# Attention output projection: operands split into a rounded part and a remainder, in two passes over the token tiles, with half sums kept in memory between the passes

## The reference

```python
def attention_mixer(hn, w_in, sink, w_out):
    proj = hn @ w_in                       # q, k, v, gate
    ...
    o = windowed_gqa_sink(q, k, v, sink)   # 16 heads in 4 groups, |t-s| <= 128
    o = (o * jax.nn.silu(gate.astype(jnp.float32))).astype(hn.dtype)
    return o @ w_out                       # 1024 x 1024 times 1024 x 1024
...
for i in range(DEPTH):
    p = layer_params[i]
    hn = rms_norm(x, p[0])
    if i % N_MIXERS == 0:
        x = x + attention_mixer(hn, *p[1:])
    else:
        x = x + deltanet_mixer(hn, *p[1:])
return rms_norm(x, final_norm)
```

## Time and profile before

| | |
|---|---|
| median of 3 runs | 1385.36 us (1385.02 to 1390.39) |
| span of the profiled execution | 1388.3 us |
| PE busy | 1324.7 us, 95% |
| DVE, ACT, POOL busy | 815.0, 684.5, 237.5 us |
| output projection on PE (L1722) | from 372.2 to 517 us of the span |

### The profile page before, as it was taken

How to read it: one execution, slowest core, us unless ns; L and a number is a source line. 1 busy time by engine, 2 the same in 40 slices (tenths; PEclk the granted TensorE clock), 3 DMA queues, 4 the chain that set the end, 5 groups by cost and what they waited for, 6 DMA issues and landing times.

```text
span 1388.3 us, 25735 instructions
## 1 busy us (share of the span) xinstructions
PE 1324.7 (95%) x9981; PEld 982.5 (71%) x9981; DVE 815.0 (59%) x2284; ACT 684.5 (49%) x1757; POOL 237.5 (17%) x164
## 2 busy tenths in 40 slices
PE   5999999999999997889999999999999999998998
PEld 4866766667644445678888888888888888865543
DVE  6335444445345426785768777787777777743243
ACT  6155464564444433437376473664746646443121
POOL 7211010111001122204032030220311303100000
PEclk9999999999999999889999999999999999999999
DMA  5110011120211122001111021110201101053121
GB/s 189 31 46 25 22 31 31 32 76 31 92 58 50 46 78 77 31 17 47 32 47 47 22 72 32 47 47 17 77 32 47 47 17 62 1 212 107 31 76 76
DMA packets 19416, 74.81 MB, mean 54 GB/s; under 512 B 3040, under 2 KB 3296, under 8 KB 17760
## 3 DMA queue, kind: packets, MB, share of 16 engines
q1 hardware_dynamic: 19296, 73.18, 15.5%
HBM read 61.04 MB, written 12.12 MB: 53 GB/s over the span
## 4 chain that ended last, share of the span: by engine, by line
PE 86%; DVE 6%; ACT 4%; issue 2%; DMA 2%; POOL 0%; SPq 0%; DVEq 0%; POOLq 0%
PE bank L1747 21%; PE bank L1650 17%; PE bank L1722 8%; PE bank L1787 4%; PE bank L1677 4%; PE bank L1762 3%; PE bank L1703 3%; PE bank L1688 3%; PE bank L1921 2%; PE bank L1839 2%; PE bank L1846 2%; PE bank L1935 2%; PE bank L1872 2%; PE bank L1938 2%; PE bank L1821 2%; PE bank L1820 2%
## 5 line engine op out<-in xcount | busy, mean ns | idle before, releaser
L1747 PE MATMUL bank<-hn_hi,w_hi 128*128 128x512 f32 x512 | 223.4, 436 | 0.5 <-ACT arena L1044 0.5
L1747 PE MATMUL bank<-hn_hi,w_lo 128*128 128x512 f32 x512 | 202.5, 396 | 0.0
L1747 PE MATMUL bank<-hn_lo,w_hi 128*128 128x512 f32 x512 | 201.3, 393 | 0.0
L1650 PE MATMUL bank<-hn_hi,w_hi 128*128 128x512 f32 x320 | 136.6, 427 | 0.5 <-ACT arena L979 0.2
L1650 PE MATMUL bank<-hn_hi,w_lo 128*128 128x512 f32 x320 | 125.8, 393 | 0.0
L1650 PE MATMUL bank<-hn_lo,w_hi 128*128 128x512 f32 x320 | 125.6, 392 | 0.0
L1722 PE MATMUL bank<-arena 128*128 128x512 f32 x256 | 119.0, 598 | 0.0
L919 POOL TENSOR_TENSOR w_lo<-arena,w_hi 128x1024 fp32r<-128x1024 f32 x24 | 61.4, 2559 | 321.8 <-ACT w_hi L1075 321.8
L1747 PEld LDWEIGHTS bank<-hn_hi,w_lo 128*128 128x128 f32 x512 | 96.8, 189 | 22.3
L1258 DVE CUSTOM_DVE_ANT_0 arena<-bank,arena 128x384 f32<-128x384 f32 (+1 forms) x128 | 70.1, 581 | 67.1 <-issue 66.8
L1747 PEld LDWEIGHTS bank<-hn_hi,w_hi 128*128 128x128 f32 x512 | 97.6, 191 | 16.4 <-ACT arena L1044 0.7
(11 more groups left out here) (234 smaller groups left out, 2653.9 us busy)
## 6 DMA issues: line engine op xcount, KB each, us to landing
arena<-in_w SPq DMA_DIRECT2D x52, 512.0 KB, 3.6
arena<-in_x SPq DMA_DIRECT2D x16, 512.0 KB, 4.7
arena<-gc_scratch SPq DMA_DIRECT2D x8, 1024.0 KB, 5.1
x_scratch<-arena SPq DMA_DIRECT2D x8, 512.0 KB, 2.6
arena<-x_scratch SPq DMA_DIRECT2D x8, 512.0 KB, 3.7
out<-arena SPq DMA_DIRECT2D x8, 512.0 KB, 2.6
oT_scratch<-arena SPq DMA_DIRECT2D x7, 512.0 KB, 5.2
arena<-oT_scratch SPq DMA_DIRECT2D x7, 512.0 KB, 8.2
```

The costliest lines, as they stand in the source:

```text
L1650: ins = te.matmul(bank[r % 2][:], wp[:, tile % 2, k], hp[:, k, hf * HALF:(hf + 1) * HALF], start=(k == 0 and m == 0), stop=(k == KT - 1 an ...
L1747: ins = te.matmul(b[:], wp[:, t % 2, k], hp[:, k, hf * HALF:(hf + 1) * HALF], start=(k == 0 and m == 0), stop=(k == KT - 1 and m == 2))
```

## The change

The output projection is made with split operands: `ornd` (ACT) copies a tile of four rows of `oT` to `oT_hi`, a ring of three; `osplit` (POOL) writes the remainder over the plain values; `wornd` and `wosplit` do the same for the eight rows of the output weights; and an item is now three fp32r matmuls. The split weights take up memory that was free before only in part: rows 0 to 3 lie in the columns of `hn_hi` and `hn_lo` of tokens 0 to 511, from the end of group 2's share of the projections on, and rows 4 to 7 in the split buffers of the input weights and in the ring of their loads.

The tiles are gone over twice (`OP_SEQ`): part 0 takes rows 0 to 3 of tiles 3, 4, 5, 6, 7, 0, 1, 2, part 1 takes rows 4 to 7 of tiles 0 to 7. So each tile has four `add`s in place of two (32 in place of 16). The half sums of tiles 3 to 7 are stored to `x1_scratch` and loaded again. `sq`, `nrm`, `ntr` and what follows now hang on part 1, with 8 items per tile: `nrm` of the tile before stands behind item 4, `ntr` behind items 6 and 8. The `Sqrt` moves from the event `sq` to the event `nrm`. `nout` writes straight into the place of `hn_lo`, `nlo` works in place, and the wait of `nout` for `nlo` is gone.

```diff
@@ -395,23 +399,31 @@
...
-            def op_items(t):
-                orders = [(hf, j) for hf in range(2) for j in (4, 5, 6, 7, 0, 1, 2, 3)]
-                if t == 0:
-                    orders = [(hf, j) for j0 in (4, 0) for hf in range(2) for j in range(j0, j0 + 4)]
-                items = [[("op", t, hf, j)] for hf, j in orders]
-                seen = [0, 0]
-                for it, (hf, j) in zip(items, orders):
-                    seen[hf] += 1
-                    if seen[hf] == KT:
-                        it.append(("add", t, hf))
-                items[-1].append(("sq", 1, t))
-                if t >= 1:
-                    items[4].append(("nrm", 1, t - 1))
-                    items[8] += [("ntr", 1, t - 1, 0), ("nout", 1, t - 1, 0), ("nhi", 1, t - 1, 0), ("nlo", 1, t - 1, 0)]
-                    items[11] += [("ntr", 1, t - 1, 1), ("nout", 1, t - 1, 1), ("nhi", 1, t - 1, 1), ("nlo", 1, t - 1, 1)]
+            def op_items(part, t):
+                items = [[("op", part, t, hf, j)] for hf in range(2) for j in range(4 * part, 4 * part + 4)]
+                for hf in range(2):
+                    items[4 * hf + 3].append(("add", part, t, hf))
+                if part == 0:
+                    after = OP_SEQ.index((0, t)) + 2
+                    if after < NT:
+                        items[-1] += [("ornd", after), ("osplit", after)]
+                else:
+                    items[-1].append(("sq", 1, t))
+                    if t >= 1:
+                        items[3].append(("nrm", 1, t - 1))
+                        items[5] += [("ntr", 1, t - 1, 0), ("nout", 1, t - 1, 0), ("nhi", 1, t - 1, 0), ("nlo", 1, t - 1, 0)]
+                        items[7] += [("ntr", 1, t - 1, 1), ("nout", 1, t - 1, 1), ("nhi", 1, t - 1, 1), ("nlo", 1, t - 1, 1)]
                 return items
+            def late_op(t):
+                split = [("ornd", NT + t), ("osplit", NT + t)]
+                if stream:
+                    stream[max(0, len(stream) - 8)] += split
+                else:
+                    put(*split)
+                stream.extend(op_items(1, t))
...
@@ -425,8 +437,14 @@
...
                     quota, share = 16, (2, 2, 2, 2, 3)
-                if 2 <= B - (A_GROUPS - 1) * NT < NT + 1:
-                    stream += op_items(B - (A_GROUPS - 1) * NT - 2)
+                late = B - (A_GROUPS - 1) * NT
+                if late == 1:
+                    put(*[(what, i) for i in range(2) for what in ("ornd", "osplit")])
+                if late == 2:
+                    for part, t in OP_SEQ[:NT]:
+                        stream.extend(op_items(part, t))
+                if 2 <= late < NT + 1:
+                    late_op(late - 2)
...
@@ -438,6 +456,9 @@
...
                     put(("exp", B))
+                    if late in (0, 1, 3, 4):
+                        for j in {0: (0, 1), 1: (2, 3), 3: (4, 5), 4: (6, 7)}[late]:
+                            put(("wornd", j), ("wosplit", j))
...
@@ -768,15 +825,25 @@
...
             sp.wait_ge(xn_done, NT)
-            for t in range(XR):
-                sp.dma_start(xr[:, t, :], x[:, t, :]).then_inc(ld_x[t], 16)
+            for part, t in OP_SEQ[:XR]:
+                sp.dma_start(xr_early(t), x[:, t, :]).then_inc(ld_x[t], 16)
+            sp.wait_ge(acc_full, acc_rank(A_GROUPS - 1, W0_TILES - 1, 0) + 1)
+            for i in range(2):
+                sp.dma_start(hn_f[:, 4 * i:4 * i + 4, 0:HALF],
+                             wout0[:, 2 * i:2 * i + 2].rearrange("p j (f n) -> p (j f) n", f=2)).then_inc(ld_wout[i], 16)
             sp.wait_ge(w0_split, A_GROUPS * W0_TILES)
-            sp.dma_start(wout[:, 4:6], wout0[:, 4:6]).then_inc(ld_wout[0], 16)
             sp.wait_ge(o_done, (A_GROUPS - 1) * NT)
-            sp.dma_start(wout[:, 6:8], wout0[:, 6:8]).then_inc(ld_wout[1], 16)
-            sp.wait_ge(acc_full, acc_rank(*LAST_PROJ) + 1)
-            sp.dma_start(wout[:, 0:4], wout0[:, 0:4]).then_inc(ld_wout[2], 16)
+            for i in range(2, 4):
+                sp.dma_start(wout_late[:, 2 * i - 4:2 * i - 2], wout0[:, 2 * i:2 * i + 2]).then_inc(ld_wout[i], 16)
+            for i in range(NT - XR):
+                t = OP_SEQ[i][1]
+                sp.wait_ge(x1_half, 2 * i + 2)
+                sp.dma_start(x1_d[:, t, :], xr_early(t)).then_inc(st_x1, 16)
+                sp.wait_ge(st_x1, 16 * (i + 1))
+                nxt = OP_SEQ[i + XR][1]
+                sp.dma_start(xr_early(nxt), x[:, nxt, :]).then_inc(ld_x[nxt], 16)
...
@@ -784,12 +851,12 @@
...
                         sp.dma_start(ring1[:, i], w1[0, i]).then_inc(ld_v[i], 16)
-                sp.wait_ge(x1_half, 2 * t + 2)
-                sp.dma_start(x1_d[:, t, :], xr[:, t % XR, :]).then_inc(st_x1, 16)
+                sp.wait_ge(x1_half, 2 * (NT + t) + 2)
+                sp.dma_start(x1_d[:, t, :], xr_of(1, t)).then_inc(st_x1, 16)
                 if t + XR < NT:
-                    sp.wait_ge(st_x1, 16 * (t + 1))
+                    sp.wait_ge(st_x1, 16 * (NT - XR + t + 1))
                     sp.wait_ge(xn_done, NT + t + 1)
-                    sp.dma_start(xr[:, t % XR, :], x[:, t + XR, :]).then_inc(ld_x[t + XR], 16)
+                    sp.dma_start(xr_of(1, t + XR), x1_d[:, t + XR, :]).then_inc(ld_x[t + XR], 16)
...
@@ -883,6 +950,19 @@
...
                                      ALU.subtract).then_inc(w0_split, 1)
+                elif e[0] == "wosplit":
+                    j = e[1]
+                    pool.wait_ge(w0_rounded, A_GROUPS * W0_TILES + j + 1)
+                    gp.tensor_tensor(wout_lo(j), wout_loaded(j), wout_hi(j).bitcast(F32), ALU.subtract).then_inc(w0_split, 1)
+                elif e[0] == "osplit":
+                    i = e[1]
+                    part, t = OP_SEQ[i]
+                    tok = slice(t * P, (t + 1) * P)
+                    pool.wait_ge(oT_rounded, i + 1)
+                    gp.tensor_tensor(oT_lo[part][:, :, tok], oT_plain[part][:, :, tok], oT_hi[:, i % 3].bitcast(F32),
+                                     ALU.subtract).then_inc(oT_split, 1)
...
@@ -959,7 +1043,22 @@
...
                     act.wait_ge(half_done, q + 1)
-                    sc.activation(hn_hi[:, 4 * hf:4 * hf + 4, t * P:(t + 1) * P], hn_half(q), ACT.Copy).then_inc(hi_done, 1)
+                    sc.activation(hn_hi[:, 4 * hf:4 * hf + 4, t * P:(t + 1) * P], hn_part(t, hf), ACT.Copy).then_inc(hi_done, 1)
+                elif e[0] == "wornd":
+                    j = e[1]
+                    act.wait_ge(ld_wout[j // 2], 16)
+                    if j >= 4:
+                        act.wait_ge(acc_full, acc_rank(*LAST_PROJ) + 1)
+                    sc.activation(wout_hi(j), wout_loaded(j), ACT.Copy).then_inc(w0_rounded, 1)
+                elif e[0] == "ornd":
+                    i = e[1]
+                    part, t = OP_SEQ[i]
+                    act.wait_ge(o_done, (A_GROUPS - 1) * NT + (t + 1 if part else 0))
+                    if i >= 3:
+                        act.wait_ge(op_full, 2 * (i - 3) + 2)
+                    sc.activation(oT_hi[:, i % 3], oT_plain[part][:, :, t * P:(t + 1) * P], ACT.Copy).then_inc(oT_rounded, 1)
...
@@ -1206,10 +1305,7 @@
...
                     dve.wait_ge(xT_done, q + 1)
-                    back = 4 if layer == 0 else 3
-                    if q >= back:
-                        dve.wait_ge(hn_done, q - back + 1)
-                    ve.tensor_tensor(hn_half(q), ntr_bank(layer, t, hf).rearrange("p (k i) -> p k i", i=P),
+                    ve.tensor_tensor(hn_part(t, hf), ntr_bank(layer, t, hf).rearrange("p (k i) -> p k i", i=P),
...
@@ -1283,20 +1379,21 @@
...
-                    t, hf = e[1:]
-                    u = 2 * t + hf
+                    part, t, hf = e[1:]
+                    u = 2 * OP_SEQ.index((part, t)) + hf
                     sl = slice(hf * HALF, (hf + 1) * HALF)
+                    row = (xr_of(1, t) if part else xr_early(t))[:, sl]
                     dve.wait_ge(op_full, u + 1)
-                    dve.wait_ge(ld_x[t], 32)
-                    ve.tensor_tensor(xr[:, t % XR, sl], bank[u % 2][:], xr[:, t % XR, sl], ALU.add).then_inc(x1_half, 1)
+                    dve.wait_ge(ld_x[t], 48 if part and t >= XR else 32)
+                    ve.tensor_tensor(row, bank[u % 2][:], row, ALU.add).then_inc(x1_half, 1)
...
@@ -1707,21 +1804,24 @@
...
-                    t, hf, j = e[1:]
-                    u = 2 * t + hf
-                    b = bank[u % 2]
-                    if j == 4:
+                    part, t, hf, j = e[1:]
+                    i = OP_SEQ.index((part, t))
+                    u = 2 * i + hf
+                    if j == 4 * part:
...
                             pe.wait_ge(x1_half, u - 1)
-                    if u == 0 and j in (0, 4, 6):
-                        pe.wait_ge(ld_wout[{4: 0, 6: 1, 0: 2}[j]], 16)
-                    if j == 6:
-                        pe.wait_ge(o_done, (A_GROUPS - 1) * NT + t + 1)
```

(13 more changed lines are left out.)

67 lines of the change are left out of this document (49 added, 18 removed).

## The result

The changed kernel takes **1391.67 us** (median of 20 executions, 1387.44 to 1395.91) against 1386.30 us for the kernel before in the same comparison (20 executions, 1384.70 to 1391.18). The ratio is 1.0034, with a 95% interval of 1.0023 to 1.0044: 0.34% slower, inside the half per cent that a measurement of this kernel can tell from no change. Forecast were 1377.0 us and a range up to 1385; the kernel lies 14.7 us above the one and outside the other. One execution of a kernel shown further down, e7_all_three, took 4487.7 us; its ratio goes by the others.

The account below looks back on a forecast made before the run. PE was taken to bound the kernel, busy for 95% of the span. 22.8 - 1.0 - 10.7 - 2.8 = 8.3 us gained: 1385.36 - 8.3 = 1377.1, called 1377.0 us; range 1370 to 1385.

Parts of the forecast that it names:

- the entry: Start of the output projection: PE waits 1.0 us for late weight rows 2 and 3; bounds 0 and 3.7.
- part 0: First pass of the output projection: the added work on DVE, ACT and POOL costs PE nothing.
- 128 items: Output projection on PE: each item takes 0.68 us instead of 0.86, saving 22.8 us in all.
- chain of the normalisation: Before part 1's normalisation transposes: PE waits seven times for add, scaling and what precedes them, 10.7 us together.
- DVE beside POOL: `norm` 1.0 us longer for tiles 0 and 2, scaling 0.4 for two others: 2.8 us; bounds 0 and 3.8.
- If `norm` came 2 us later than I think: A case for part 0: each of its four full steps would lose about 1 us; not charged.
- the second rival: PE's clock falls in the long waits for tiles 0 and 2, 3.8 us together: 1380.9 us; chance 0.20.
- My third rival: PE's clock falls in every wait, seven times 1.9 us: 1390.4 us; chance 0.04.
- going between fp32 work and split items: On PE: costs nothing new, since steps of groups 0 to 2 have such changes too.
- What would show it: Signs: items 0.68 us apart, seven PE waits before normalisation transposes, none in part 0, table load before `exp` only in block 7.
- The three for wrong: PE idle before items, released by `add` or POOL; 0.63 us matmuls behind waits; output projection beginning later than some 372 us.

Follow-up runs that it names:

- e7_all_three: The changed kernel with the edits of e1, e5 and e6 together: 1379.74 us, ratio 0.9928 to the kernel before.
- e1: The changed kernel with POOL starting each pair of `wosplit` only when the same step's `norm` is done: 1386.71 us, ratio 0.9997 to the kernel before.
- e2: The changed kernel with each `wosplit` cut into four POOL instructions of 256 columns: 1385.91 us, ratio 0.9995 to the kernel before.
- e8: The changed kernel with `norm`'s four instructions also adding up their rows into a spare column: 1384.00 us, ratio 0.9967 to the kernel before.
- e4: The changed kernel with 9, 15 and 6 unread matmuls ahead of the first transposes of tiles 0, 2 and 6: 1385.64 us, ratio 0.9988.
- e10: The changed kernel with e5, e6, e8, tile 7's scaling ahead of tile 6's second half, and two attention transpose groups side by side per step: 1371.08 us.
- e5: The changed kernel with the transposes of a tile's normalisation two items later: 1384.63 us, ratio 0.9976 to the kernel before.
- e6: The changed kernel with `exp` of blocks 6 and 7 ahead of the last two items: 1384.42 us, ratio 0.9980 to the kernel before.

## Why the prediction was wrong

It was wrong by 14.7 us, and on the other side of no change: the gain of 8.3 us became a loss of 5.4 (6.4 in the traced stretch). Term by term, with the stretch as the measure. The larger part of the miss, 7.7 of 14.4 us, is the clock, which stood at nothing in the sum; the waits at the entry and in part 0 are 5.5, the items 2.1, and the chain took 0.9 less than forecast. PE's idle times in the rows count from the modelled end of the last matmul, 0.39 us behind its start, though the next could have started after 0.23: each wait costs 0.16 more than its row says, and that is added here.

| term of the sum | predicted | measured |
|---|---|---|
| 128 items | -22.8 | -20.7 |
| entry, waits | +1.0 | +3.2 |
| entry, clock | 0 | +1.7 |
| part 0 | 0 | +3.3 |
| chain of the normalisation, with DVE beside POOL | +13.5 | +12.6 |
| clock behind its waits | 0 | +6.0 |
| sum | -8.3 | +6.1 |

The sum of the right column stands against the 6.4 us of the trace. The clock's share is the length of the windows shown behind the waits, times what their granted clock lacks of 1: 1.7 at the entry, then 1.7, 2.6 and 1.7.

- **"Charged nothing" for part 0, and the entry, failed on one step: the price of DVE beside POOL.** I read from the earlier trace rows that `norm` takes 2.42 us beside POOL in place of 1.41, and made 1.0 us of it, a fixed surcharge, and charged it in part 1 alone. But in that row a single one of the four instructions is held, from 424.18 to 425.61, until POOL's ends at 425.40. The price is the rest of POOL's instruction, and then a whole one for each further instruction of DVE, for as long as POOL has work: `wosplit` has two of 2.4 us right behind one another and `osplit` behind them. The waits of 0.60, 0.94 and 1.13 us at the entry are all `norm`'s; the one that I had charged there, for rows 2 and 3 of the weights, didn't come, since PE reached them late. I had the durations ("POOL then needs twice 2.4 us") and the moment ("in the same moment as `norm`") on the page, for `osplit`; for `wosplit`, which ACT releases 1.1 us after `exp`, the two never met in one sentence. e1, e2 and e8 show the cause three ways. The trace of before had the price as well, in group 0, on a sum of two tensors of 128x4 that takes 0.16 us elsewhere:

```profile
134.50 1.98 DVE L1266 TENSOR_TENSOR arena<-arena 128x4 f32<-128x4 f32 x1
```

```profile
134.07 2.38 POOL L884 TENSOR_TENSOR w_lo<-arena,w_hi 128x1024 fp32r<-128x1024 f32 x1 [17.73 <-ACT w_hi L969]
```

It ends with POOL's instruction, at 136.5. The rule was to be had, too, and I cited the weaker of two places. The Trainium skill (SBUF — State Buffer, Who interferes with whom) says that whichever of the two issues first holds the shared ports for the whole instruction and that the other is blocked, not slowed. By that rule `norm` waits for 4.8 us of POOL in four steps, and the trace agrees: 5.65 to 6.70 us.
- **A step that I had priced and thought away.** "If `norm` came 2 us later than I think, each of its four full steps would lose about 1 us." It came 4.3 and 5.3 us later in two of them, and each lost 1.51 (1.67 by the measure above), less than that price makes of 4 to 5 us.
- **The chain of the normalisation came out close, in part by luck**: waits before the transposes seven times and nowhere else in part 1. The rows have 2.77, 0.23, 4.18, 0.23, 1.01, 1.01 and 2.10 us, 11.5 together; predicted were 2.1, 0.5, 4.0, 0.6, 1.0, 1.0 and 1.5, and 2.8 for POOL. POOL's share was larger than the 2.8 and the chain's own shorter than the 10.7, and the two errors cancel. `norm` is 1.0 us longer than alone for tiles 0 and 2, the scaling 0.35 for tiles 4 and 5 (1.10 in place of 0.75) and 1.28 for tile 6, where it runs beside `w1split` (2.03 at 517.99): 4.0 together. What is left of the waits is 7.5, 8.6 by the measure: 0.66 for tiles 4 and 5 in place of 1.0, 3.2 for tile 2 in place of 4.0.
- **The clock was the second rival, and had 0.20.** I let it fall twice at 1.9 us; in the trace it fell four times, 7.7 us in all, behind waits of 0.94, 2.77, 4.18 and 2.10 us. My third rival, a fall in every wait, is not what happens either: behind 1.01 and 1.51 us it stayed. e4 agrees with what the rows say the falls are worth, within its interval. As a rival of its own beside a sum that already had waits of 3 and 5 us in it, it was given too little: with no row between 1.2 and 6 us to say that the clock holds, the central sum should have carried half of it.
- **128 items** gave 2.1 us less. I took 0.680 us between items from the earlier trace rows; in the output projection they lie 0.70 apart (22 in a row take 5.12 us from 403.55 on, 0.233 per matmul against 0.227), and the step of block 3 saves 2.59 us for 16 items, 0.162 each. What makes these matmuls 3% slower wasn't tried; it isn't the output projection alone, since the input projections from 372.57 to 374.66 lie 0.232 apart too. The prediction's ground for charging nothing for going between fp32 work and split items was wrong: the steps of 16 items before were all plain fp32 and had no such changes. That it cost nothing all the same (e10: 0.09 us lost on an item, 0.09 gained on the transposes) was luck.
- **What would show it** held as a list of signs. The three for wrong came: PE idle before items, released by `add`; matmuls of 0.63 us behind waits; and a projection that begins 4.3 us later, at 376.5.

## What to carry to other kernels

Work put on POOL is free only if no instruction of DVE that waits for POOL, and on whose result PE waits, runs beside it: look at what DVE does at the moment when POOL is released, and count up to one whole POOL instruction for each such instruction of DVE. Cutting POOL's instructions, releasing them behind DVE's, or a form of DVE's that doesn't wait each took the loss at the entry and in part 0 away. And when a change makes PE's work shorter than a chain that it used to hide, the clock that falls behind the waits can add half as much again (6.0 to 12.6 us here); giving the chain two more items (e5, 8.0 us by the ratios) and taking the squares out of it (e6, 7.5) helped alike.

## What the runs showed of the hardware

- A DVE `tensor_scalar` of 256 to 1024 columns in fp32 from SBUF to SBUF waited for the running POOL instruction to end: four of them took 1.14 to 1.41 us alone, 2.4 to 2.6 beside POOL instructions of 0.72, 3.19 beside two of 1.3, 5.65 and more beside two of 2.4. The sum of two 128x4 tensors in SBUF waited likewise (1.14 us for 0.15). A `tensor_scalar` of 128x1 did not (0.14 us at 517.22, with 2.3 us of POOL's instruction still to come), nor did `add`, which has one operand in PSUM (0.69 us at 385.03, with 1.1 us of POOL's instruction to come, and as much alone). The form of `tensor_scalar` that also writes a row sum never waited: 0.61 us for 384 columns and 0.47 for 256 (32 instructions in group 3 of e8), where the plain one takes 0.42 and 0.35.
- How long PE stands idle doesn't decide alone whether its clock falls. Behind 0.94 us at 366 it fell in the traces of after and e6, not in those of e4 and e5; behind 2.10 us it fell in after, e1, e2 and e8, not in e6; behind 2.77 it fell (after, e2), behind 2.73 (e7) it stayed; behind 3.39 us it stayed (e5), behind 3.34 it fell, in the same trace and in that of e7. Behind 4.17 and 4.18 us it fell each time (after, e1, e2), behind 1.01 and 1.51 never.
- For the changed kernel the clock goes with most of the scatter: its 20 executions lie between 1387.44 us at a mean granted clock of 0.989 and 1395.91 at 0.983, 8.5 us apart, and 0.006 of the span is 8.4 us.
